# Three 512-column matmuls into an unused bank ahead of the products of two blocks in each plain GEMM stage

## The reference, cut to what matters

```python
y = x + branches(norm(x) @ w_in, norm(x) @ w_gate) @ w_o       # block 1, mixer
y = y + gate * (act(norm(y) @ w_up) @ w_down)                   # block 1, feed-forward, 8192 wide
z = y + mixers(norm(y) @ w_in_2) @ w_out_2                      # block 2, mixer
z = z + gate * ((silu(g) * v) @ w_down_2)                       # g, v = taps(norm(z) @ w_up_2), 5632 wide
```

## Time and profile before

| | |
|---|---|
| Median of three executions | 3175.56 us (3174.21 to 3181.29) |
| Span of the profiled execution, first to last instruction | 3166.6 us |
| What lies around the span, if that execution took the median | 8.96 us |
| Mean granted TensorE clock | 0.995 |
| TensorE busy | 98% of the span |
| Chain of waits that ended last | TensorE 90%, VectorE 6%, DMA 1%, ScalarE 1% |

### The profile page before, as it was taken

How to read it: one execution, slowest core, us unless ns; L and a number is a source line. 1 busy time by engine, 2 the same in 40 slices (tenths; PEclk the granted TensorE clock), 3 DMA queues, 4 the chain that set the end, 5 groups by cost and what they waited for, 6 DMA issues and landing times.

```text
span 3166.6 us, 55394 instructions
## 1 busy us (share of the span) xinstructions
PE 3099.8 (98%) x23974; PEld 2933.4 (93%) x23974; DVE 2369.1 (75%) x2843; ACT 1334.2 (42%) x1459; POOL 1.8 (0%) x10
## 2 busy tenths in 40 slices
PE   7999999999999999999999999999999999999997
PEld 6899999999999999998988999989889989999996
DVE  4799876688887889899978765644767666767766
ACT  3343344444444443333463334422455444344444
POOL 0000000000000000000000000000000000000000
PEclk9999999999999999999999999999999999999999
DMA  9864444498894887777855763354343475655743
GB/s 395 333 216 168 162 158 149 173 352 344 328 366 160 311 306 273 269 264 288 297 186 212 274 256 139 134 217 160 120 147 134 174 265 187 226 213 201 258 177 136
DMA packets 106417, 722.62 MB, mean 228 GB/s; under 512 B 11677, under 2 KB 15389, under 8 KB 27197
## 3 DMA queue, kind: packets, MB, share of 16 engines
q1 hardware_dynamic: 100368, 703.64, 59.6%
q10 hardware_dynamic: 5806, 15.43, 1.6%
HBM read 712.41 MB, written 6.55 MB: 227 GB/s over the span
## 4 chain that ended last, share of the span: by engine, by line
PE 90%; DVE 6%; DMA 1%; ACT 1%; issue 1%; ACTq 0%; DVEq 0%
PE gemm L1040 40%; PE gemm L1049 19%; PE gemm L1076 12%; PE gemm L1079 6%; PE mix L1040 1%; DVE sb_parts L1781 1%; PE mix L1291 1%; PE mix L1571 1%; DMA sb_arena<-x_t 1%; ACT sb_parts L539 1%; DMA sb_raw<-stream 1%; DVE sb_arena L1836 1%; PE gemm L1207 1%; PE mix L1049 1%; PE mix L1150 1%
## 5 line engine op out<-in xcount | busy, mean ns | idle before, releaser
L539 ACT ACTIVATE sb_parts<-sb_raw 128x2048 fp32r<-128x2048 f32 (+2 forms) x489 | 899.6, 1842 | 1464.1 <-PE gemm L1049 958.9
L1781 DVE TENSOR_TENSOR sb_parts<-sb_raw,sb_parts 128x2048 fp32r<-128x2048 f32 (+2 forms) x489 | 1071.9, 2193 | 301.7 <-PE gemm L1049 149.9
L1040 PE MATMUL gemm<-op_h,sb_parts 128*128 128x256 f32 x7232 | 876.5, 278 | 1.1 <-ACT sb_parts L539 0.6
L1040 PEld LDWEIGHTS gemm<-op_h,sb_parts 128*128 128x128 f32 x7232 | 853.2, 188 | 2.5 <-ACT sb_parts L539 1.0
L1049 PE MATMUL gemm<-op_h,sb_parts 128*128 128x256 f32 x3616 | 455.4, 278 | 0.0
L1049 PEld LDWEIGHTS gemm<-op_h,sb_parts 128*128 128x128 f32 x3616 | 434.8, 188 | 0.2 <-DVE sb_parts L1781 0.2
L1076 PE MATMUL gemm<-op_up,sb_parts 128*128 128x512 f32 x1728 | 418.0, 392 | 3.0 <-DVE op_up L2410 3.0
L1076 PEld LDWEIGHTS gemm<-op_up,sb_parts 128*128 128x128 f32 x1728 | 315.3, 188 | 65.4 <-DVE op_up L2410 4.8
L1079 PEld LDWEIGHTS gemm<-op_up,sb_parts 128*128 128x128 f32 x1728 | 218.3, 188 | 10.5
L1762 DVE CUSTOM_DVE_ANT_0 sb_raw<-sb_raw,sb_arena,sb_vec 128x2048 f32<-128x2048 f32 x96 | 224.3, 2348 | 1.1
L1079 PE MATMUL gemm<-op_up,sb_parts 128*128 128x256 f32 x1728 | 220.6, 278 | 0.0
(11 more groups left out here) (360 smaller groups left out, 3340.3 us busy)
## 6 DMA issues: line engine op xcount, KB each, us to landing
sb_raw<-stream SPq DMA_DIRECT2D x597, 1024.0 KB, 5.0
sb_raw<-stream SPq DMA_DIRECT2D x64, 704.0 KB, 4.1
sb_arena<-stream SPq DMA_DIRECT2D x14, 1024.0 KB, 7.9
sb_arena<-stream SPq DMA_DIRECT2D x10, 768.0 KB, 8.2
sb_raw<-stream SPq DMA_DIRECT2D x6, 768.0 KB, 7.2
sb_arena<-c_rows ACTq DMA_DIRECT2D x3, 1024.0 KB, 8.4
bias_rows<-sb_arena ACTq DMA_DIRECT2D x1, 2304.0 KB
sb_arena<-x_t ACTq DMA_DIRECT2D x4, 512.0 KB, 19.1
```

Source lines behind the costliest of these rows:

```text
L539: act.activation(parts[:, b % 2, 0, 0:kt, :], slot_of(slot)[:, 0:kt, :], ACT.Copy).then_inc(hi_ready, 1)
L1040: ins = pe.matmul(out, l, r, start=(opens and i == 0 and x is xh), stop=False, skip_group_check=True)
L1781: dve.tensor_tensor(parts[:, b % 2, 1, 0:kt, :], slot_of(slot)[:, 0:kt, :], parts[:, b % 2, 0, 0:kt, :].bitcast(F32), ALU.subtract).then_i ...
```

## The change

`three_wide` issues three matmuls of 512 columns into `mix3` with the block's first high weight tile and the input's first k-tile. Nothing reads what they write. `product` gets two hooks: `ahead`, behind the waits for the high part and ahead of the 32 high products, and `between`, behind the wait for the low part and ahead of the 16 low products. `gemm_T_wide` is `gemm_T` with `three_wide` in both places. It is used for blocks 3 and 4 of `a_f`, for blocks 1 and 2 of `w_o`, and for the first two blocks of the first `plain_round` of a section with `opH`. A wait on `cols_read` is added ahead of block 3 of `a_f`.

```diff
+            def three_wide(b, op):
+                for _ in range(3):
+                    pe.matmul(M[3][:, :], parts[:, b % 2, 0, 0, :], op[:, :, 0, :].rearrange("p a s -> p (a s)"), start=True, stop=True)
...
                 hi, lo = (parts[:, :, 0], parts[:, :, 1]) if pair else (parts[:, b % 2, 0], parts[:, b % 2, 1])
+                ahead()
...
                         pe.wait_ge(taken[slot], uses + 1)
+                    between()
...
+            def gemm_T_wide(b, op, it=0):
+                product(b, [features(bank(b)[:, 0:S], op)], it, ahead=lambda: three_wide(b, op), between=lambda: three_wide(b, op))
...
             pe.wait_ge(cg_read, 1)
+            pe.wait_ge(cols_read, KT)
             for i in range(3, 16):
-                gemm_T(gb("a_f", i), opH)
+                if i in (3, 4):
+                    gemm_T_wide(gb("a_f", i), opH)
+                else:
+                    gemm_T(gb("a_f", i), opH)
...
                 for j in range(4):
-                    gemm_T(gb(section) + 4 * r + j, op, it, 4, kt=kt, waits=waits if r == j == 0 else {})
+                    if op is opH and it == 0 and j in (0, 1):
+                        gemm_T_wide(gb(section) + 4 * r + j, op)
+                    else:
+                        gemm_T(gb(section) + 4 * r + j, op, it, 4, kt=kt, waits=waits if r == j == 0 else {})
 
             for k in range(KT):
-                gemm_T(gb("w_o", k), opG, waits={KT - 1: (merged_tile, KT)} if k == 0 else {})
+                if k in (1, 2):
+                    gemm_T_wide(gb("w_o", k), opG)
+                else:
+                    gemm_T(gb("w_o", k), opG, waits={KT - 1: (merged_tile, KT)} if k == 0 else {})
```

More of the change, by code:

```diff
@@ L1019, in _, with product @@
             norms, sq_parts, sum_adds = [0], [0], [0]
-            def product(b, pieces, it=0, dn=0, pair=False, later=False, waits={}, ready={}):
+            def three_wide(b, op):
+                for _ in range(3):
+                    pe.matmul(M[3][:, :], parts[:, b % 2, 0, 0, :], op[:, :, 0, :].rearrange("p a s -> p (a s)"), start=True, stop=True)
+            def product(b, pieces, it=0, dn=0, pair=False, later=False, waits={}, ready={}, ahead=lambda: None, between=lambda: None):
                 both = range(b, b + 2) if pair else range(b, b + 1)
```

## The result

Over 18 timed executions of each kernel the changed one took 3192.38 us (3180.72 to 3209.92) and the kernel before 3177.76 us (3161.8 to 3201.14). The ratio is 1.0049, 95% interval 1.0032 to 1.0066: slower by 15.6 us (10.2 to 21.0) by that ratio. The forecast was 3183.3 us in a range of 3171 to 3196, and "slower by over 0.2%" as the likeliest case. Of the 9.1 us by which the time itself was missed, 2.2 are the kernel before's own: its median over 18 is 3177.76, over the first three it was 3175.56.

A forecast was written before the change was run, and what follows sets the result against it. TensorE, busy 98% of the span, was taken as the bound, with the 256-column pitch the only thing to pay: 27.5 us of wides less 19.7 us back is +7.8 us, from 3175.6 to 3183.3 us, range 3171 to 3196.

The forecast's parts named there:

- The cost: In ten stages, 120 wide matmuls at 228.8 ns each, all path on TensorE: 27.5 us, 2.75 us per twelve.
- The table of exits: Length of the last 512-column matmul sets the pitch behind it: 394 ns fast, 388 or 392 slow.
- P, Q and R: Starts of three wides in a slow stream: 392, 394, 388; 397, 397, 392; 397, 394, 394 ns; only the third turns fast.
- a_f: 592 matmuls turned fast give back 2.63 us, bounds 0 and 2.63, VectorE keeping up by 0.07 us a block.
- up1_0 and up2_2: Slow stages turned fast, from the first and from the second triple: 2.56 and 4.56 us back.
- w_o: DMA is next in line, so 1.7 us back, bounds 0 and 3.20; stage no shorter than now.
- A: Rival, 0.18: not slower; up1_1 to up1_3 slow in timed executions, made fast through up1_0, 10.2 us back, 3173.1 us.
- up2_0's +3.70 us back: Stage entered by P, fast from the second triple on, 832 matmuls: 3.70 us back.
- The terms of up2_1 to up2_3: up2_1 and up2_2 slow, turned fast, 4.56 us back each; up2_3 already fast, nothing back, 2.75 us cost.
- B: Rival, 0.12: triples turn no slow stream fast, so all is cost: 3203.0 us.
- C: Rival, 0.05: triples turn nothing fast and also leave fast streams slow: 3218 us.
- D: Rival, 0.05: the wides stand in seven stages and not ten, 8.2 us less: 3175.1 us.

The follow-up runs named there:

- one_two: Kernel before plus one wide matmul ahead of up1_3's first high products and two ahead of up2_3's, no others; ratio 0.9998 (0.9982 to 1.0014).
- knock: rotate_lean plus one, two and three wides ahead of the fifth block of up2_1, up2_2 and up2_3; single execution, no ratio; 101.76, 101.76, 97.92 us behind them.
- rotate: Kernel before plus three triples sixteen narrow matmuls apart in a_f, merge, up1_0 and up2_0 to up2_3 (63 wides); 3175.95 us, ratio 0.9959.
- fast_only: Changed kernel with triples only in up1_1, up1_2, up1_3 and up2_3 (48 wides); 3196.46 us, ratio 1.0019 against the kernel before.
- rotate_up1_1: rotate_lean with the spaced triples moved from up1_0 to up1_1, profiled twice; 3170.12 us, ratio 0.9965 against the kernel before.
- after: First profiled execution of the changed kernel, with its 120 wides, against the kernel before; 3192.39 us.
- rotate_lean: rotate without a_f's triples and with only two triples each in up2_1 to up2_3 (45 wides); 3171.88 us, ratio 0.9948 against the kernel before.

## Why the prediction came out as it did

**Right.** *The cost:* twelve wides add 2.06 us to a fast stage beyond its first triple and 2.75 in all, as in up1_1, which took 89.10 us from the end of the first triple against 87.04. *The bound* was TensorE's pitch alone; no wait appeared that could be put down to the triples. *The table of exits* (394 fast, 388 and 392 slow) and the entries P, Q and R fit every triple that stood in an unbroken stream, in the ten profiles that have triples, and the shorter groups of one_two and knock; the shift by narrow matmuls, which was taken from single stamps, was put to the test by rotate and held. *a_f:* 543 matmuls in 61.54 us, so VectorE kept up, and the stage with its twelve wides ended within 0.1 us of what it had been: +0.12 was forecast. *up1_0 and up2_2* gave back 2.6 and 4.5 us, as forecast, against the first profile of before. Only in part right was *w_o:* the forecast gave DMA as next in line and 1.7 us back. The stream went fast at the first triple, and by single start stamps every later block of w_o ran at 113.3 ns within itself. So w_o did pull through at 113, but for one wait of 0.5 us: a sign that the forecast had named, since it held DMA to be next in line. From its first matmul to its last w_o took 90.83 us for 90.81, so 2.7 us came back and not 1.7. Behind it the norm's first matmul waited 0.8 us for VectorE, and up to there the stage is 0.7 us longer than before, where 1.05 was forecast. The waits from 870 to 957 us:

```profile
ACT sb_parts L539 <- DMA sb_raw<-stream: 10.4, 6, 3.2
...
PE mix L1175 <- DVE sb_arena L1895: 0.8, 1, 0.8
...
PE gemm L1047 <- ACT sb_parts L539: 0.5, 1, 0.5
```

**The step that failed** is to cost each stage by the state in which one execution had met it, "against the profiled span ... with the same 9.0 us around it". It took the draw of one execution for that of the kernel. In three later profiles time and span of one execution differ by 1.8 us (3192.39 and 3190.6, 3181.95 and 3180.2, 3206.17 and 3204.4), and in no later execution by 2.0 or more. With 1.8, the profiled execution of before took about 3168.4 us and stood 7 us below the median it was set against, and 9 below that of all 18 executions. So some 7 of the 9.0 us were luck, and the largest piece is the merge: fast there, slow in all six other profiles without triples in it, 9.4 us. That piece by itself moves nothing in the sum, since the change does not touch the merge and the forecast came back to the median by adding the 9.0. But it says that the states in the earlier trace rows, from which the sum was made, were not the usual ones. The forecast named the merge ("the merge's alone would be worth 9") as a width of the range, and not as a sign of this. Its argument against *A*, "span plus 9 us is the median", is none: the 9.0 was had by taking the span from the median.

**The term that it mis-sized** comes of this step: up2_0's +3.70 us back, on the entry P seen once. In the eleven profiles in which up2_0 was slow, the entry was P four times, Q four and R three; for up1_0 it was P three times, Q five and R five of thirteen. From Q nothing is given back. Both profiles of the changed kernel had Q in up2_0, and one had it in up1_0: with 3.70 and half of 2.56 off the gains, the sum is 7.8 + 3.7 + 1.3 = 12.8 us, inside the measured 10.2 to 21.0. With the shares of all profiles (4 of 11 and 5 of 13) it is 7.8 + 1.3 + 1.0 = 10.1, just below the interval. The terms of up2_1 to up2_3 hold on average: in the eight profiles without spaced triples in up2_0, up2_2 was always met slow, up2_1 was met fast in four (4.6 us less back than forecast, each time) and up2_3 slow in four (as much more). This is worked out afterwards from few profiles; which stages make up the other few us, the timed executions don't say.

**Where the profiles' 24.0 us lie.** From the start stamps of both profiles, each stage counted from its first triple: the ten stages with triples add 11.1 us, where the forecast's +7.8 and up2_0's gain not had, +3.7, make 11.5. The merge adds 9.4, and the branch blocks ahead of it, in the same stream and slow like it, 1.1. m_q, also without triples, adds 1.7, and m_v 1.6 in its first half and -2.4 near its end. The start of the kernel, up to 54 us, adds 1.0, and what is left is 0.5. So 12.9 of the 24.0 lie in stages that the change does not touch, and comparing the two profiles alone would have put the change at half as much again as the 15.6 us measured.

**The rivals.** *A* said that the timed executions have up1_1 to up1_3 slow. It was half right on the fact (slow in six of ten profiles, leaving out fast_only and the two of rotate_up1_1, where triples or a stall at them set up1_1) and wrong on the way. It held that up1_0, once fast, hands that on. In the five profiles without a stall in down1_0, four came to up1_1 fast (up1_0 left by R, or fast in after) and one slow (left by Q): so the conversion from R buys nothing there, since R leads to a fast up1_1 anyway, and from Q there is no conversion. For P it stays open: all three profiles with P in up1_0 stalled in down1_0. And in eight profiles down1_0 stalled. In three of these up1_0 was left fast, as in after: up1_1 was slow all the same in two (rotate, knock) and fast in one (rotate_lean). The stall in rotate ends with a late DMA, by the rows above. But the DMA share from 1066 to 1140 us is 0.97 in rotate and 0.98 in the kernel before, which did not stall: there is no slack in either, and what makes a block late in one execution and not in another isn't shown. *B* (nothing converts) and *C* (fast streams left slow) are refuted by the first profile: a_f, w_o, up1_0, up2_2 and up2_3 were met slow and turned fast, up1_1 to up1_3 and up2_1 met fast and kept so. C's worry is real for one or two wides, as knock shows, and not for three. *D* is refuted by the 120 matmuls.

**One gap for one width.** The runs go on disagreeing with it: knock has 101.76 and 97.92 us for the same 864 matmuls at one clock and one DMA share. The Trainium skill (TensorE: Matmul & The Clock Gate, "Back-to-back issue gap") has 109.2 ns as the isolated gap of a warm array at 256 columns, 94.3 us for the 864 as an estimate, below both.

**What stays open.** Why three wides make a period, and what in TensorE holds the two pitches apart, no run shows. What decides the pitch behind a stall isn't known either, only that it can come out otherwise than before it and than in another execution. Why rotate_up1_1 gained 11 us and not 16 wasn't settled: with the merge, up1_1 to up1_3 and up2_0 to up2_3 fast in both profiles, the cause may lie in the draws of before on that chip, whose median was 3183.88 us against 3187.68 on rotate_lean's.

## What to carry to other kernels

When the same code runs at two pitches in one profile, profile it two or three times before costing anything: a single profile is one draw, and two of one kernel differed by 13.6 and 13.8 us here, nearly what the change was worth. Set an execution's span against its own time and not against a median; a gap of 9 us where others have 2 says how lucky that execution was. If a steady state can be flipped by a short odd sequence, design the sequence so that it ends well from every entry, and put it behind the last place where a stall can redraw the state: forty triples laid out without regard to the entry cost 5 parts in a thousand here, and fifteen laid out with it won 3 to 5, in rotate_up1_1 with a third of the spread.

## What the runs showed of the hardware that was not expected

A stream of 256-column matmuls with a weight load each, at a granted clock of 1.00, has two steady pitches, 113.33 and 117.78 ns, and can hold either for 2112 matmuls (239.36 or 248.74 us). One 512-column matmul in a fast stream is enough to make the 864 behind it slow; two do the same; three leave it fast. Behind a stall the pitch can change, and executions of one kernel differ in it: that makes up 11.1 of the 13.6 us between two profiles of the kernel before (merge 9.4, m_q 1.7; up2_1 and up2_3 cancel). w_o is 1.7 us longer too, but at 117.78 ns in both; TensorE waited 0.9 us there for ScalarE's rounding and 0.7 us behind it for VectorE. The spread of 39 us among 18 executions of the kernel before is of the size of such draws added up, though only profiled executions show which stages drew what.
